# A decoder layer on one core: table pieces, decode batches at other attention steps, output weights ahead of the last value slabs

## The reference

```
mod = silu(c) @ ada_w + ada_b                       # six shift/scale/gate vectors
h = rmsnorm(x)*(1+sc1)+sh1 ; z = h @ w_in           # columns q | k | v | u
att = dilated windows (128,1),(512,4),(2048,16) over 8 heads x 64, T5 bias, merged by softmax
ssm = S5 scan of 32 groups x 16 channels, 64 complex states; gelu; per-group GLU
x = x + g1 * (concat(rmsnorm(att), rmsnorm(ssm)) @ w_out)
h2 = rmsnorm(x)*(1+sc2)+sh2
x = x + g2 * MoE(h2)                                # top 1 of 4 groups, top 2 of 4 SwiGLU experts
y = rmsnorm(x)
```

## Time and profile before

| | |
|---|---|
| runs, us | 903.39, 908.45, 911.05 (median 908.45) |
| profiled execution | 910.8 us, its span 909.0 us |
| busy share of the span | PE 81%, PE weight loads 47%, DVE 34%, ACT 19%, POOL 19% |
| mean granted TensorE clock | 0.871 |
| DMA | 212.08 MB, mean 233 GB/s |

### The profile page before, as it was taken

The page is one execution under the profiler, slowest core; times in us unless marked ns, Lnnn a source line. Parts: engine busy times, 40 slices in busy tenths (PEclk is TensorE's granted clock), DMA queues, the critical chain, the costliest instruction groups (busy, mean ns, idle before and its releaser), DMA issues.

```text
span 909.0 us, 10439 instructions
## 1 busy us (share of the span) xinstructions
PE 739.9 (81%) x3994; PEld 425.2 (47%) x3994; DVE 306.3 (34%) x785; ACT 169.5 (19%) x416; POOL 169.9 (19%) x274
## 2 busy tenths in 40 slices
PE   2399998499599999884799844999999999999800
PEld 1286687388265665552345443444443444444200
DVE  3733137444145565620146354111011111111038
ACT  1331000024123342550212110011011111111032
POOL 1325228402323332320000001000000000000063
PEclk8588999699569899996799855999999999999955
DMA  9960287062910802667514396784989999999352
GB/s 323 383 236 22 105 276 280 6 239 93 399 47 19 342 12 77 260 252 245 178 50 134 120 331 246 247 306 161 401 290 403 407 397 397 402 396 400 154 196 98
DMA packets 83129, 212.08 MB, mean 233 GB/s; under 512 B 3516, under 2 KB 9948, under 8 KB 80997
## 3 DMA queue, kind: packets, MB, share of 16 engines
q1 hardware_dynamic: 69254, 179.89, 53.8%
q0 software_dynamic: 5472, 19.16, 5.9%
q10 hardware_dynamic: 8352, 12.34, 3.9%
HBM read 197.18 MB, written 17.86 MB: 237 GB/s over the span
## 4 chain that ended last, share of the span: by engine, by line
PE 66%; DVE 10%; DMA 9%; POOL 7%; issue 4%; ACT 2%; SPq 1%; ACTq 0%; DVEq 0%; POOLq 0%
PE ps L2245 19%; PE ps L2248 12%; PE ps L2153 7%; PE ps L1909 5%; PE ps L1789 5%; PE ps L1878 3%; DMA ct_im<-in_ct_im 3%; DMA wo_attention<-in_w_out 3%; PE ps L1940 2%; PE ps L1942 2%; PE ps L1960 2%; PE ps L1974 1%; PE ps L2003 1%; DMA mod_d<-modsb 1%; POOL yg L777 1%
## 5 line engine op out<-in xcount | busy, mean ns | idle before, releaser
L2245 PE MATMUL ps<-ering,xgT 128*128 128x512 f32 x256 | 115.1, 604 | 2.5 <-ACT xgT L794 1.7
L1909 PE MATMUL ps<-hT,ring 128*128 128x272 f32 x384 | 91.7, 402 | 15.3 <-ACT qkT L794 15.3
L1909 PEld LDWEIGHTS ps<-hT,ring 128*128 128x128 f32 x384 | 74.4, 195 | 31.9 <-ACT qkT L794 15.8
L2245 PEld LDWEIGHTS ps<-ering,xgT 128*128 128x128 f32 x256 | 48.5, 193 | 63.4 <-issue 60.1
L2248 PE MATMUL ps<-ering,xgT 128*64 128x512 f32 x320 | 70.6, 595 | 1.2 <-ACT xgT L794 1.2
L761 POOL DMA_INDIRECT xg<-h_d,gidx x13 | 12.4, 951 | 242.8 <-PE ps L1789 210.1
L2245 PE MATMUL ps<-ering,aT 128*128 128x512 f32 x128 | 56.2, 593 | 0.0
L1802 PE MATMUL ps<-ring,silu_c 128*32 128x128 f32 x768 | 27.4, 309 | 24.2 <-DMA ring<-in_ada_w 24.2
L2153 PE MATMUL ps<-wo_attention,mixT 128*128 128x512 f32 x64 | 33.2, 679 | 13.8 <-DMA wo_attention<-in_w_out 13.8
L2248 PEld LDWEIGHTS ps<-ering,xgT 128*64 128x64 f32 x320 | 22.6, 137 | 44.6 <-issue 43.2
L1702 DVE SCALAR_TENSOR_TENSOR a_t<-a_t,ps 128x512 f32<-128x512 f32 x13 | 8.9, 687 | 96.7 <-ACT a_t L794 96.7
(11 more groups left out here) (426 smaller groups left out, 1122.0 us busy)
## 6 DMA issues: line engine op xcount, KB each, us to landing
ering<-in_w_gate SPq DMA_DIRECT2D x16, 2048.0 KB, 17.2
ering<-in_w_up SPq DMA_DIRECT2D x16, 2048.0 KB, 16.7
ering<-in_w_down SPq DMA_DIRECT2D x16, 2048.0 KB, 20.8
ring<-in_ada_w SPq DMA_DIRECT2D x12, 2048.0 KB, 12.8
ring<-in_cache_k SPq DMA_DIRECT2D x8, 1792.0 KB, 10.6
ring<-in_cache_v SPq DMA_DIRECT2D x8, 1792.0 KB, 11.5
ring<-in_w_in SPq DMA_DIRECT2D x4, 2048.0 KB, 23.9
y_d<-ysb ACTq DMA_DIRECT2D x26, 256.0 KB, 6.1
```

What stands on the lines that cost most here:

```text
L1909: ins = mm(out, r[:, 512 * k + P * c:512 * k + P * (c + 1)], hT[:, k, cols], start=k == 0, stop=k == KD - 1)
L2245: return mm(out, lhsT=lhs, rhs=ering[slots[0]][:, cols], start=k == 0, stop=k == n - 1)
```

## The change

- **Tables.** `doubling` takes a range of tiles. The steps for m = 1, 2, 4 all follow z = 0; m = 8 and half of 16 follow z = 1; m = 32 is cut in two (after z = 3 and 4), m = 64 in four (after z = 5 to 8).
- **Modulation wait.** DVE's wait for `s_modst` moves from ahead of the attention loop to steps 3 and 4.
- **Decode batches.** The values of batch 0 go from steps 24 to 27 to steps 19 to 22, its result from 29 to 24. The keys of batch 1 go from the GLU stage into steps 28 to 31; its softmax comes ahead of `att_out` on DVE, its transposes ahead of the first GLU half.
- **Loads.** `wo_attention` goes ahead of the last four value slabs; the S5 half gets a place of its own (`wo_ssm`) and follows it. `mod3S`, `rw` and `rb` now wait for the values of batch 1. The first four expert slots are issued after two tiles of x instead of after all five.
- **Order behind the GLU.** `wo(0, 0)` and `wo(1, 0)` stand on the two sides of the last GLU half; all values come after both; then the merge, `wo(0, 1)` and only then `att_t(QT)`. `s5_sum(q)` now stands directly behind the second half of group q.

The core of the diff:

```diff
-KEYS_AT = {9 + q: q for q in range(4)}
-VALUES_AT = {24 + i: i for i in range(4)}
-SOFTMAX_AT, EXP_AT, TURN_AT, COPY_AT, OUT_AT = 14, 15, 17, 18, 29
+KEYS_AT = {9 + q + 19 * g: (g, q) for g in range(2) for q in range(4)}
+VALUES_AT = {19 + i: i for i in range(4)}
+SOFTMAX_AT, EXP_AT, TURN_AT, COPY_AT, OUT_AT = 14, 15, 17, 18, 24
...
-        for i in range(IT_KV + 2, IT_WO):
+        for i in range(IT_KV + 2, IT_KV + 12):
             item(i)
         sp.wait_ge(s("bu"), STT)
         sp.dma_start(wo_a[:, :].rearrange("p (k n) -> p k n", k=4), wo_v[:, 0:4, :]).then_inc(s("woal"), 16)
+        sp.wait_ge(s("yp"), STT)
+        sp.dma_start(wo_s[:, :].rearrange("p (k n) -> p k n", k=4), wo_v[:, 4:8, :]).then_inc(s("wosl"), 16)
+        for i in range(IT_KV + 12, IT_WO):
+            item(i)
...
-        sp.wait_ge(s("yp"), STT)
+        sp.wait_ge(s("perm"), 4)
+        sp.wait_ge(s("dOp"), NSEQ)
+        sp.wait_ge(s("statest"), 16)
         for t in range(TDEC):
             sp.dma_start(mod3S[t:NS:TDEC, :, :].rearrange("p v (c j n) -> p (v c) j n", c=2, j=4),
                          mod_rows_seq(3, 2)).then_inc(s("mod3"), 16)
...
+        PIECES = {0: ((1,), (2,), (4,)), 1: ((8,), (16, 0, 8)), 2: ((16, 8, 16),), 3: ((32, 0, 8),), 4: ((32, 8, 16),),
+                  **{5 + n: ((64, 4 * n, 4 * n + 4),) for n in range(4)}}
...
-        for b in (1, 2):
-            dve.wait_ge(s_modst[b], 64)
...
+            if st in (3, 4):
+                dve.wait_ge(s_modst[st - 2], 64)
...
+        dec_softmax(1)
         dve.wait_ge(s("gel"), STT)
         for j in range(QT):
             att_out(j)
...
+        s5_tokens(0)
+        dec_probs_t(1)
+        s5_glu(0, 0)
+        s5_tokens(1)
+        s5_glu(0, 1)
+        s5_sum(0)
+        s5_glu(1, 0)
...
+        s5_sum(2)
+        s5_glu(3, 0)
         wo(0, 0)
         s5_glu(3, 1)
-        s5_sum(2)
+        wo(1, 0)
+        s5_sum(3)
         for part in range(4):
             dec_values(1, part)
...
+            wo(p, 1)
+            if p == 0:
+                att_t(QT)
```

More of the change, by code:

```diff
@@ L342, in _build @@
     sq = at("ssm_squares", [P, NTOK], QK + 4096)
-    wo_a = at("wo_attention", [P, 4 * D], E)
+    wo_a, wo_s = at("wo_attention", [P, 4 * D], E), at("wo_ssm", [P, 4 * D], E + 16384)
     x2 = at("x2", [P, NT, D], QK)
     mod3P = at("mod3P", [P, 3, D], TAB)
-    mod3S = at("mod3S", [NS, 3, D], E + 16384)
+    mod3S = at("mod3S", [NS, 3, D], QK + 20480)
     gate2P, gate2S = at("gate2P", [P, D], QK + 24576), at("gate2S", [NS, D], TAB)
@@ L556, in _, with weights @@
         which = {r: r for r in range(STATIC)}
[L557 to L565, removed]
+        def weights(m):
+            r, w = W_ITEMS[m]
+            if m == 4:
+                sp.wait_ge(s("woA"), NT)
+                sp.wait_ge(s("woS"), NT)
             elif m == 6:
@@ L575, in _ @@
             sp.dma_start(*expert(which[r], w, m % R2)).then_inc(efull[m % R2], 16)
+        x_rows(0)
+        x_rows(1)
+        for m in range(R1):
+            weights(m)
+        for p in range(2, NT):
+            x_rows(p)
+        for m in range(R1, len(W_ITEMS)):
+            weights(m)
         sp.wait_ge(s("eid"), 1)
@@ L994, in _ @@
         ssm_out(1)
-        dec_probs(1)
         gate_tanh(2, 0)
@@ L1342, in _ @@
             z_half(z)
-            if z < 7:
-                doubling(1 << z)
+            for piece in PIECES.get(z, ()):
+                doubling(*piece)
+        dve.wait_ge(s("tables"), 1)
         dve.wait_ge(s("modg"), N_ADA)
@@ L2104, in s5_sum @@
             ins.then_inc(s("ssp"), 1)
-        for st in range(NST + 2, LAST_STEP):
-            s5_step(st)
-        dec_keys(1, 0)
-        dec_keys(1, 1)
-        for j in range(QT):
-            att_t(j)
-        s5_tokens(0)
-        dec_keys(1, 2)
-        s5_glu(0, 0)
-        s5_tokens(1)
-        s5_glu(0, 1)
-        dec_keys(1, 3)
-        s5_glu(1, 0)
-        s5_tokens(2)
-        s5_glu(1, 1)
-        s5_sum(0)
-        dec_probs_t(1)
-        s5_glu(2, 0)
-        s5_tokens(3)
-        s5_glu(2, 1)
-        s5_sum(1)
-        s5_glu(3, 0)
         def wo(p, half):
@@ L2135, in wo @@
                 pe.wait_ge((s("woa"), s("wog"))[half], p)
-            if half:
-                wait_item(pe, IT_WO)
-            else:
-                pe.wait_ge(s("woal"), 16)
-            r = ring[IT_WO % R1] if half else wo_a
+            pe.wait_ge(s("wosl" if half else "woal"), 16)
+            r = wo_s if half else wo_a
             if j == QT:
@@ L2155, in wo @@
             ins.then_inc((s("woA"), s("woS"))[half], 1)
+        for st in range(NST + 2, LAST_STEP):
+            s5_step(st)
+        for j in range(QT):
+            att_t(j)
+        s5_tokens(0)
[5 more added lines that the diff above has]
+        s5_glu(1, 0)
+        s5_tokens(2)
+        s5_glu(1, 1)
+        s5_sum(1)
+        s5_glu(2, 0)
+        s5_tokens(3)
+        s5_glu(2, 1)
+        s5_sum(2)
+        s5_glu(3, 0)
         wo(0, 0)
         s5_glu(3, 1)
-        s5_sum(2)
+        wo(1, 0)
+        s5_sum(3)
         for part in range(4):
             dec_values(1, part)
-        s5_sum(3)
         pe.wait_ge(s("dOe"), 2)
-        pe.wait_ge(s("ytok"), 4)
         for g in range(2):
@@ L2167, in _ @@
         ins.then_inc(s("attSp"), 1)
-        att_t(QT)
-        pe.wait_ge(s("gluo"), NT)
+        pe.wait_ge(s("gated"), 8)
         def h2_t(p):
@@ L2198, in _ @@
         for p in range(NT):
-            for half in range(2):
-                if p or half:
-                    wo(p, half)
+            if p >= 2:
+                wo(p, 0)
+            wo(p, 1)
+            if p == 0:
+                att_t(QT)
             if p:
```

91 lines of the change are left out of this document (47 added, 44 removed).

## The result

| | before | changed |
|---|---|---|
| median of 20 runs, us | 909.53 (903.39 to 920.1) | 917.94 (909.1 to 930.36) |
| profiled execution, its span, us | 910.8, 909.0 | 909.1, 907.3 |
| mean granted clock | 0.871 | 0.890 |

The ratio changed to before is 1.0089, 95% interval 1.0066 to 1.0112: about 8 us slower, where 3.4 us faster was forecast. The ratios here, unlike the medians, leave out executions that lie over 1.5% above the fastest of their kernel: of the changed kernel two, of experiment 2 two, of 5 one, of 10 one (1,921 us, unexplained), and of the kernel before one in each comparison. The profiled execution of the changed kernel is the shortest of its 20 and stands 1.7 us ahead of the one of before. A single trace would have told the wrong story, so the same kernel was run again (median 915.77) and gave a trace of span 912.3 us. Both are read here.

The account below looks back on a forecast made before the run. The prediction took the kernel to run mostly over PE's lines, with a 13.8 us wait for wo_attention. Terms 0.3 + 8.3 - 12.0 = -3.4 gave 907.4 us on the profiled execution, 905.0 against the median; range 896 to 917.

Parts of the forecast that it names:

- Tables and modulation wait: Ahead of the attention loop: tables cut in pieces -1.6 us, earlier first exponential by the moved modulation wait -2.4.
- Keys and values in the loop: Attention loop: values of batch 0 five steps earlier +0.5 us, keys of batch 1 in steps 28 to 31 +6.5.
- rival F: Attention loop: PE's idle time in the last steps absorbs the keys; -6.5 us more, 898.5; chance 0.12.
- Loop end to the first GLU half: From the attention loop's end to the first GLU half: 16.4 us against 13.6 before, +2.8.
- GLU groups: First GLU half to wo(0, 0): 25.9 us, one group near the lower clock's price, two at the upper, the last half.
- A: The forecast itself: granted clock about 0.5 in the first GLU group, 1.00 in the second; 905.0 us; chance 0.36.
- C: GLU stage: the clock stays down throughout; 11.7 us slower than the forecast, 916.8; chance 0.22.
- wo(0, 0) to the end of the values: From the start of wo(0, 0) to the last values: 26.5 us against 18.2 before, +8.3.
- Values to h: From the values' end to the first transposes of h: 20.4 us, -12.0; one product less, the hole closed.
- Rival D: Behind the values: mod3S's last part and rw, rb come some 3 us too late for the join; 907.8; chance 0.13.
- Sum: Total up to the transposes of h: +0.3 at wo(0, 0)'s start, +8.3, -12.0, giving -3.4 us.

Follow-up runs that it names:

- experiment 2: Changed kernel with SP issuing wo_ssm and the last four value slabs only after the GLU weights have landed; 906.01 us, ratio to before 0.9962.
- experiment 5: Changed kernel with the keys of batch 1 in steps 29 to 32 in place of 28 to 31; 907.29 us, ratio to before 0.9991.
- experiment 10: Kernel before with only wo_attention issued ahead of the last four value slabs; 901.06 us, ratio to before 0.9932.
- experiment 11: Kernel before with only the tables in pieces and the modulation's wait moved to steps 3 and 4; 899.7 us, ratio to before 0.9926.
- experiment 7: Changed kernel with the keys of batch 1 back in the GLU stage, their softmax and transposed probabilities behind them; 894.04 us, ratio to before 0.9857.
- experiment 9: Changed kernel with batch 1's keys back in the GLU stage, sums one group later, values ahead of wo(1, 0); 884.6 us, ratio to before 0.975.
- experiment 6: Changed kernel with 18 products that nobody reads added in PE's waits ahead of and in the GLU stage; 908.82 us, ratio to before 1.0019.
- experiment 4: Changed kernel with the values of batch 1 ahead of wo(1, 0) and the last sums; 911.5 us, ratio to before 1.0033.

## Why the prediction was wrong

**Tables and modulation wait** (-4.0 together): of the right size. PE's wait in the projection fell from 15.33 to 13.59 us in the changed kernel's first trace, and the exponential moved from 248.78 to 246.38 there, 243.48 in the second (-2.4 and -5.3). The two terms don't simply add: ACT loads its table at 245.08 us in the first trace, as before, since it had been issuing a store until then.

**Keys and values in the loop** (+7.0): nearly right, though the two traces hide it. From the first exponential to the last `head_out` it is 127.6 us before, and 131.1 and 131.7 now, +3.8 in the mean. But the loop of before is long in its own trace for the clock at its start (experiment 11). The four other traces without these keys in the loop (experiments 7, 9, 10, 11) have 122.9 to 123.5; against them the keys cost about 8 us, the earlier values of batch 0 nothing (123.3 and 122.9 us with them, 123.5 and 123.2 without), and rival F is not borne out for these steps. One step later (experiment 5) the loop is 2 to 3 us longer than theirs, partly by a better clock in one stretch, so a part of F may hold there. The quarters wait 1.3 to 2.2 us for their slab in all six traces that have them in steps 28 to 31. I had this as the upper end of a range; that the clock goes down for 12 us behind the longer of these waits I had not. Three of the six have it, none of them a trace of the changed kernel; whether it adds to the spread of that kernel's runs, 909 to 930 us, is not shown.

**Loop end to the first GLU half** (16.4 us, +2.8 against before): this is the step that failed. It measured 23.0 and 23.4, +9.4 and +9.8. What I saw of the transfers was that 4.2 MB of weights and four slabs would have time to land. What I left out is who else loads in that time: POOL fetches the GLU weights exactly then, twice 256 KB, and my own rows had the hint: the half already waited 1.51 us for them before. Experiment 2 shows the cause: with these weights in time the stretch takes 16.0 us, against my 16.4. And I left out that the keys' place sets the slabs' time: with the keys in the loop, SP issued the slabs 15 us earlier than before (experiment 7). The clock, at the lower level in this stretch, was as forecast, but it isn't what held the half: experiment 6 had 1.00 there up to 400 us and still took 22.3. One reading in this step was wrong too: before had three of the four quarters ahead of the half, 6.3 us by their rows, and not eight quarters' worth; nothing in the sum hung on it.

**GLU groups** (11.2 + 6.8 + 6.8 + 1.1): the structure was right, 6.8 us to the hundredth at the upper clock. The clock was the choice between A and C, and I gave A 0.36 and C 0.22. The first trace is A (22.8 us; a little under its 25.9, as the first group took 8.2 and not 11.2), the second C (30.4; C's price had been 34.4), and so are those of experiments 2 and, in its later groups, 7. C expected a clock of 0.5 throughout; the second trace has 0.67, as part of each group still ran at the upper level. Experiment 6 shows that it is PE's idling that keeps the clock down. Why the same instructions run as A in one execution and as C in another stays open. The Trainium skill, page "TensorE: Matmul & The Clock Gate", section "What's actually happening", says that the default state is throttled and that activity releases it. Both traces of the changed kernel agree: the first half, behind 7.5 and 9.0 us of idle PE, takes 2.18 us at the lower clock, where it took 1.19 before. The sentence doesn't tell A from C.

**wo(0, 0) to the end of the values** (26.5): 27.8 and 29.8. The wait ahead of `wo(1, 0)` was there (3.19 us), but the product behind it ran at the lower clock, 8.7 to 8.8 for the 7.03 that I took, and in the second trace `wo(0, 0)` did too (8.84).

**Values to h** (20.4): 19.3 in both, 12.9 us gained. Right (by its own rows the term was -11.8, not -12.0), and the reason that the change isn't worse than it is. Rival D had no part in it: the four issues of `mod3S` took 2.93 us together, not 2.9 each; the times of the earlier trace rows were taken behind a full queue.

**Sum.** Up to the transposes of h the second trace is 6.3 us behind before: -5.3 (start) + 4.1 (loop) + 9.8 (to the first half) - 1.0 (groups and the hole) + 11.6 (to the end of the values) - 12.9. The forecast had -3.4 there; of the 9.7 us between, 7.0 lie in the way to the first half, 4.5 in the groups and 3.3 behind `wo(0, 0)`, both at the lower clock; start, loop and last stretch give 5 back. In the first trace the sum is -1.3; the largest part of the difference is the 7.6 us between its groups and those of the second. At the end of the execution the second trace is 3.3 us behind before, and the runs say 8; the trace of before has the long loop and is slower than its median, the second trace faster than its own, so the two traces alone understate the loss. The hole of 13.8 us was removed in full. In its place stand about 8 us for the keys in the loop, 7.5 to 9 us of waiting for the GLU weights, 7 us of waits for squares, and the lower clock. The time lies near C's 916.8, but C alone doesn't explain it, and its full price wasn't paid; the range's upper end stood 0.9 us short because no case held the GLU weights' wait and the clock together.

## What to carry to other kernels

When a large transfer comes earlier, be it moved in the list or released earlier because what used its buffer was moved, list every load that any queue issues in the stretch it now fills, the small ones first, with its landing time and who waits for it: a 256 KB load that took 3 us took 11 behind 9 MB. An order on PE that puts a reader directly behind its producer costs the wait, and here in some executions the clock after it; a group later, the same instructions were 10 us faster. And one profiled execution may be the best of twenty: take a second one before a difference of 1% is explained.

## What the runs showed of the hardware

- A wait of 2.1 to 2.2 us for a key slab, inside a stretch of otherwise busy PE, was followed by a granted clock near 0.50 for some 12 us (experiments 2, 4 and 6); waits of 1.3 us at the same place were not, in three traces. Waits of 2.29 us in the GLU stage of the changed kernel's first trace weren't either, so the length of the wait alone doesn't decide.
- Filling waits with useless products made the kernel 6.5 us faster, some 4 us to either side.
- Two loads of 256 KB landed in 8.1 and 10.5 us (8.6 and 10.9 in the second trace) with 9 MB of other transfers issued some 10 us ahead of them, and in 2.9 to 3.4 us without them (before, experiments 2, 7 and 10).
- Four small issues (`mod3S`) behind 9 MB of queued transfers held SP's list for 33 us (experiment 10), and 2.93 us where the DMA engines had nothing else to do (changed kernel).
